# Prompt attention rows multiplied by their reciprocal sums on GpSimd instead of VectorE

## The chip, the cores and the metric

The kernel runs on one core of one Trainium2 chip. A core has a matrix engine (TensorE, PE in the profile), a vector engine (VectorE, DVE), an activation engine (ScalarE, ACT), GpSimd (POOL) and a queue engine for transfers (SyncE, SP). They run side by side and are tied together by semaphores only. The metric is the device time of one launch in microseconds. A time for comparison is a median of several runs; the profile is one more execution with the hardware profiler on.

## The reference

The program computes one inference step of a two-layer hybrid decoder for 512 prompt tokens and 8 samples of 8 tokens, all in float32. Each layer has three mixers (a causal pooling mixer, a gated linear recurrence and a latent attention), their gated merge, and a gated feed-forward network with a short convolution. The change touches one step of the attention of the prompt, eight heads over 512 tokens:

```python
s = einsum(q_lat, ckv) + einsum(q_pe, kpe)
s = where(q_pos >= k_pos, s * MLA_SCALE, -inf)
p = softmax(s, axis=-1)
o = einsum(p, ckv)
```

The softmax is computed as the maximum of a row, the exponential of the row less its maximum (with the sum of the row beside it), the reciprocal of the sum, and the product of the row with that reciprocal. The last product is the subject here.

## The kernel before

The prompt attention of a layer is cut into 32 blocks, numbered n = 0 to 31: four pairs of heads, four chunks of 128 queries in each pair, two heads in each chunk. Block n has 128 queries in the partitions and, because of the causal mask, 128, 256, 384 or 512 keys in the columns, two blocks of each width in turn. So the pattern of widths repeats every eight blocks, and a period here means eight blocks (one pair of heads).

Each block passes through these steps, with the program's names:

- TensorE makes the scores in PSUM (`att_score`, L930 and L931 for the mask).
- VectorE takes the negative maximum of each row out of PSUM (`att_stats`, L2035).
- ScalarE writes the exponentials to `probs`, one of four SBUF buffers (`r` in the profile), and the row sums to `stat` (`att_softmax`, L1632).
- VectorE takes the reciprocal of the sums, 128x1 (L2043), and multiplies the row by it, in place (L2045). Both are in `att_normalise`.
- TensorE transposes the row in pieces of 128 columns (`att_turn`, L939). ScalarE copies the result to SBUF (`att_take`, L1623). TensorE multiplies it with the values (`att_values`, L951), for two blocks at a time.

The order on each engine is written out by hand and never changes at run time. TensorE runs, for each n: scores of block n+3, transposes of block n, and after each odd n the values of the blocks two and three before. VectorE runs, for each n: reciprocal and product of block n, row maxima of block n+3; after n = 10, 18 and 26 it also copies a finished pair of heads out of PSUM (L2050). ScalarE runs: exponentials of block n, copy of the transposes of block n-2. An engine that waits for a semaphore holds up all that stands behind it.

The product signals `att_probs`, for which the transposes of the same block wait, and which a reciprocal four blocks later waits for too. GpSimd has nothing to do in this stage: its queue holds a subtraction (L2810) ahead of it, and behind it the first product of the recurrence (`value_blocks`, L2682), which waits for work after the attention of the samples. The sample attention follows the prompt attention on TensorE and has its own product on VectorE (L2265), which stays.

Of the kernel before, what the change touches and what calls it, by code (L numbers as in the profile page):

```python
# [20 lines left out]
ALU = mybir.AluOpType  # L21
# [4 lines left out]
P = 128  # L26
# [34 lines left out]
N_ATT_BUFS = 4  # L61
N_CHUNK = SEQ // CHUNK
# [114 lines left out]
N_ATT = MLA_HEADS * N_CHUNK  # L177
# [20 lines left out]
def build(nc, xT_in, w_stream, small_in, att_in, const_in, pages_in, kpe_in, page_table, pool_state,  # L198
          hgrn_state, conv_state, yT, ckv_out, kpe_out, pool_out, hgrn_p_out, hgrn_s_out, conv_out):
    with ExitStack() as ctx:  # L200
# [56 lines left out]
        probs = [r1[:, o + i * SEQ:o + (i + 1) * SEQ] for i in range(N_ATT_BUFS)]  # L257
# [142 lines left out]
        def att_stat(n, which):  # L400

            c = 4 * (n % N_ATT_BUFS) + which
            return stat[:, c:c + 1]
# [63 lines left out]
        def signal(name, per_layer):  # L467
            return Signal(sem(name), per_layer)
# [56 lines left out]
        att_recip = signal("att_recip", N_ATT)  # L525
        att_probs = signal("att_probs", N_ATT)
# [141 lines left out]
        def level_differences(eng, h, first=0, end=len(LEVELS)):  # L668

            for half, out, t0, t1 in levels(h, first, end):  # L670
                lo, hi, _ = parts(out, half)
                _, lhi, mid = parts(logf[:, h, t0:t1], half)
                alo, _, _ = parts(log_k[:, h, t0:t1], half)
                mid = mid.broadcast_to([P, (t1 - t0) // (2 * half), half])
                eng.tensor_tensor(hi, lhi, mid, ALU.subtract)
                ins = eng.tensor_tensor(lo, alo, mid, ALU.add)
            return ins

        def level_scaled(eng, h, first=0, end=len(LEVELS)):

            for half, out, t0, t1 in levels(h, first, end):
                _, hi, _ = parts(out, half)
                _, qhi, _ = parts(q_hg[:, h, t0:t1], half)
                ins = eng.tensor_tensor(hi, hi, qhi, ALU.mult)
            return ins
# [1301 lines left out]
        def _(dve):  # L1987
# [42 lines left out]
            def att_stats(l, n):  # L2030
                keys = (n % (2 * N_CHUNK) // 2 + 1) * P
                dve.wait_ge(*att_scores.at(l, n + 1))
                if n >= N_ATT_BUFS:
                    dve.wait_ge(*att_exp.at(l, n - N_ATT_BUFS + 1))
                dve.tensor_reduce(att_stat(n, 0), att_bank(n)[:, 0:keys], AX_X, ALU.max, negate=True  # L2035
                                  ).then_inc(att_max.sem, 1)

            def att_normalise(l, n):
                keys = (n % (2 * N_CHUNK) // 2 + 1) * P
                dve.wait_ge(*att_exp.at(l, n + 1))  # L2040
                if n >= N_ATT_BUFS:
                    dve.wait_ge(*att_probs.at(l, n - N_ATT_BUFS + 1))
                dve.reciprocal(att_stat(n, 3), att_stat(n, 2)).then_inc(att_recip.sem, 1)  # L2043
                dve.wait_ge(*att_recip.at(l, n + 1))
                dve.tensor_scalar(probs[n % N_ATT_BUFS][:, 0:keys], probs[n % N_ATT_BUFS][:, 0:keys], att_stat(n, 3), None,  # L2045
                                  ALU.mult).then_inc(att_probs.sem, 1)

            def take_head_pair(l, j):
                dve.wait_ge(*att_pv.at(l, N_CHUNK * (j + 1)))
                dve.tensor_copy(o_mla[:, j, 0:SEQ], pv_bank(j)).then_inc(att_out_taken.sem, 1)  # L2050
# [84 lines left out]
            with dve.Fori(0, DEPTH) as l:  # L2135
# [105 lines left out]
                        dve.tensor_copy(v_hg[0:rows, m, :], slot(TILE_HI + m)[0:rows, 0:512]).then_inc(tile_dve.sem, 1)  # L2241

                for n in range(N_ATT):
                    att_normalise(l, n)
                    if n + N_ATT_BUFS - 1 < N_ATT:
                        att_stats(l, n + N_ATT_BUFS - 1)

                    if n >= 10 and n % (2 * N_CHUNK) == 2:
                        take_head_pair(l, n // (2 * N_CHUNK) - 1)
# [410 lines left out]
        def _(pool):  # L2660
# [14 lines left out]
            def ends_scaled(l, h):  # L2675
                pool.wait_ge(*ends_exp.at(l, h + 1))
                pool.tensor_tensor(decayed[:, h % 2, 0, :], decayed[:, h % 2, 0, :], q_hg[:, h, :], ALU.mult
                                   ).then_inc(lev_ready.sem, 1)

            def value_blocks(l, h):  # L2680

                pool.tensor_tensor(v_blocks,  # L2682
                                   v_hg[0:SAMPLES, 4, h * P:(h + 1) * P].unsqueeze(1).broadcast_to(
                                       [SAMPLES, S_PAIRS, P]),
                                   own_rows.unsqueeze(2).broadcast_to([SAMPLES, S_PAIRS, P]), ALU.mult
                                   ).then_inc(blocks_ready.sem, 1)
# [119 lines left out]
            with pool.Fori(0, DEPTH) as l:  # L2806

                pool.wait_ge(*prep_dve.at(l, 8))
                pool.wait_ge(*q_rope.at(l, 2))
                pool.tensor_tensor(log_k, log_k, logf, ALU.subtract).then_inc(log_k_ready.sem, 1)  # L2810

                pool.wait_ge(*smp_new_rows.at(l, 2))
                pool.wait_ge(*smp_cols_taken.at(l, S_PAIRS))
                pool.wait_ge(*tile_act.at(l, taken(TILE_HQ + 3)))
                pool.wait_ge(*taken_at(l, TILE_HI + 4))
                pool.wait_ge(*log_k_ready.at(l, 1))
                value_blocks(l, 0)
                pool.wait_ge(*pool_d_ready.at(l, POOL_GROUPS))
                differences(l, 2)

                pool.wait_ge(*hg_upd.at(l, N_CHUNK + 2))
                ends(l, 2)
                value_blocks(l, 1)
                ends_scaled(l, 2)
                differences(l, 3)

                pool.wait_ge(*hg_upd.at(l, 2 * (N_CHUNK + 2)))
                ends(l, 3)
                value_blocks(l, 2)
                ends_scaled(l, 3)  # L2830

# [301 lines left out]
```

## Time and profile before

| | |
|---|---|
| median of 3 runs | 2267.76 us (2265.02 to 2270.11) |
| the profiled execution, its own time | 2267.23 us |
| span of the profiled execution | 2265.4 us |
| mean granted clock of TensorE | 0.994 |
| TensorE busy | 2196.5 us, 97% of the span |
| VectorE busy | 1183.0 us, 52% |
| GpSimd busy | 993.9 us, 44% |
| ScalarE busy | 526.5 us, 23% |

The span runs from the first to the last instruction; the launch adds 1.8 us around it. TensorE has work nearly always, so a change can move the time in two ways: by TensorE's own work, or by the gaps in which it waits. The prompt attention runs from about 158 to 209 us in the first layer and from about 1282 to 1333 us in the second. All stamps below are microseconds from the start of the span.

### The profile page before, as it was taken

To read this page: it belongs to the slowest core of one execution; us is meant where nothing else is said; L and a number is where in the kernel's file an instruction comes from. 1 tells how busy PE (TensorE), PEld (TensorE's weight loads), DVE (VectorE), ACT (ScalarE), POOL (GpSimd) and SP (SyncE) were. 2 spreads that over 40 slices of the span, in tenths; PEclk is the share of its full clock that TensorE was granted. 3 is DMA by queue.
4 is the path that set the end of the run, shared out by engine and by line. 5 is a ranking of instruction groups with operands and counts; after the bars stand their busy time and mean duration, and the time that the engine had idled before them with its cause. 6 is when DMAs were issued, how large, how long until landed. Compare 5 with 4: busy or idle time off the path is not lost.

```text
span 2265.4 us, 36978 instructions
## 1 busy us (share of the span) xinstructions
PE 2196.5 (97%) x11856; PEld 1691.6 (75%) x11856; DVE 1183.0 (52%) x2124; ACT 526.5 (23%) x1112; POOL 993.9 (44%) x1128
## 2 busy tenths in 40 slices
PE   8999999999999999999899999999999999999996
PEld 6775777777777777777676757777777777777775
DVE  0545666333578666661216346753335776666523
ACT  1434343111132001100134343531111311001002
POOL 0000046667665666633300000465666566666251
PEclk9999999999999999999999999999999999999998
DMA  5322113222132222222132221131221322222211
GB/s 210 101 84 66 43 63 114 84 75 77 55 126 75 74 76 88 71 72 77 38 133 86 75 67 42 63 133 66 84 84 57 120 80 74 74 74 70 96 52 42
DMA packets 51616, 183.54 MB, mean 81 GB/s; under 512 B 7234, under 2 KB 27970, under 8 KB 37762
## 3 DMA queue, kind: packets, MB, share of 16 engines
q1 hardware_dynamic: 50882, 178.49, 22.9%
q10 hardware_dynamic: 576, 3.06, 0.3%
q8 instruction: 84, 1.38, 0.2%
q14 instruction: 74, 0.61, 0.1%
HBM read 172.35 MB, written 9.18 MB: 80 GB/s over the span
## 4 chain that ended last, share of the span: by engine, by line
PE 91%; DVE 3%; issue 2%; POOL 1%; ACT 1%; SPq 1%; DMA 0%; DVEq 0%; ACTq 0%
PE ps L1219 25%; PE ps L1139 22%; PE ps L1261 16%; PE ps L898 12%; PE ps L1513 3%; PE ps L930 1%; PE ps L1427 1%; PE ps L1291 1%; PE ps L951 1%; PE ps L939 1%; PE ps L919 1%; PE ps L1079 1%; PE ps L983 1%; PE ps L1413 1%; PE ps L1057 1%
## 5 line engine op out<-in xcount | busy, mean ns | idle before, releaser
L1219 PE MATMUL ps<-lq,mreg 128*128 128x288 f32 x1008 | 251.3, 406 | 0.0
L898 PE MATMUL ps<-xT,wring 128*128 128x288 f32 (+2 forms) x960 | 236.5, 408 | 2.7 <-DVE o_mla L2289 1.4
L1219 PEld LDWEIGHTS ps<-lq,mreg 128*128 128x128 f32 x1008 | 191.5, 190 | 52.9
L1623 ACT ACTIVATE r<-ps 128x288 f32<-128x288 f32 (+7 forms) x264 | 112.8, 431 | 480.1 <-PE ps L1139 257.0
L898 PEld LDWEIGHTS ps<-xT,wring 128*128 128x128 f32 x960 | 183.2, 191 | 54.4 <-issue 2.2
L1219 PE MATMUL ps<-xT,wring 128*128 128x288 f32 x672 | 169.8, 406 | 0.0
L1219 PEld LDWEIGHTS ps<-xT,wring 128*128 128x128 f32 x672 | 127.7, 190 | 35.3
L1139 PE MATMUL ps<-r,kbuf 128*128 128x288 f32 x576 | 143.6, 406 | 0.0
L1139 PEld LDWEIGHTS ps<-r,kbuf 128*128 128x128 f32 x576 | 109.4, 190 | 30.2
L1952 ACT ACTIVATE r<-r 128x592 f32<-128x592 f32 x44 | 30.7, 697 | 428.5 <-DVE r L2594 428.5
L2783 POOL TENSOR_TENSOR kbuf<-o_mla 128x288 f32<-128x288 f32 x42 | 33.3, 792 | 207.8 <-DVE o_mla L2558 207.8
L1623 ACT ACTIVATE o_mla<-ps 128x288 f32<-128x288 f32 (+1 forms) x108 | 45.2, 420 | 326.2 <-PE ps L1261 214.5
L2810 POOL TENSOR_TENSOR kbuf<-kbuf,lq 128x2304 f32<-128x2304 f32 x2 | 10.1, 5054 | 248.4 <-DVE side L2221 248.4
L2682 POOL TENSOR_TENSOR mreg<-vbuf,const 64x512 f32<-64x512 f32 x8 | 8.3, 1032 | 251.8 <-PE ps L1541 243.1
L2594 DVE SCALAR_TENSOR_TENSOR r<-r,small 128x592 f32<-128x592 f32 x88 | 106.4, 1209 | 12.4 <-DVE r L2591 12.0
L2591 DVE SCALAR_TENSOR_TENSOR r<-r,small 128x592 f32<-128x592 f32 x88 | 104.5, 1188 | 12.4 <-DVE r L2588 9.7
L1139 PE MATMUL ps<-xT,wring 128*128 128x288 f32 x384 | 97.0, 406 | 0.0
L1261 PE MATMUL ps<-r,side 128*128 128x288 f32 x372 | 92.7, 407 | 0.8 <-DVE r L2605 0.8
L1219 PE MATMUL ps<-lq,wring 128*128 128x288 f32 x336 | 88.3, 406 | 0.0
L1219 PE MATMUL ps<-xT,mreg 128*128 128x288 f32 x336 | 88.3, 406 | 0.0
L1139 PEld LDWEIGHTS ps<-xT,wring 128*128 128x128 f32 x384 | 73.0, 190 | 20.2
L1139 PE MATMUL ps<-lq,r 128*128 128x288 f32 x336 | 87.4, 406 | 0.0
(435 smaller groups left out, 4540.6 us busy)
## 6 DMA issues: line engine op xcount, KB each, us to landing
wring<-w_stream SPq DMA_DIRECT2D x100, 1024.0 KB, 4.9
side<-w_stream SPq DMA_DIRECT2D x18, 704.0 KB, 4.5
r<-pages_in SPq DMA_DIRECT2D x80, 128.0 KB, 2.2
vbuf<-w_stream SPq DMA_DIRECT2D x12, 512.0 KB, 3.7
r<-w_stream SPq DMA_DIRECT2D x12, 512.0 KB, 3.6
wring<-w_stream SPq DMA_DIRECT2D x8, 704.0 KB, 4.1
r<-w_stream SPq DMA_DIRECT2D x6, 704.0 KB, 4.1
mreg<-pages_in SPq DMA_DIRECT2D x32, 128.0 KB, 2.1
```

Source lines behind the costliest of these rows:

```text
L898: mm = pe.matmul(out[0:w.shape[-1], a * 512:a * 512 + hi - lo], w, x[:, lo:hi], start=(k == 0), stop=(k == len(pairs) - 1))
L919: mm = pe.matmul(slot(tile + j)[:, a * 512:a * 512 + hi - lo], w, xT[:, k, lo:hi], start=(k == 0), stop=(k == KD - 1))
L930: pe.matmul(att_bank(n)[:, 0:keys], q96[:, j, e, t0:t0 + P], k96[:, j, e, 0:keys], start=True, stop=False)
L1139: mm = pe.matmul(banks[name], ws[:, k * P:(k + 1) * P], xs[:, k, :], start=(k == 0), stop=(k == n - 1))
L1219: mm = pe.matmul(up_sum[name], ws[:, k * P:(k + 1) * P], xs[:, k, :], start=(k == 0), stop=(k == HK - 1))
L1261: mm = pe.matmul(res_bank(which, m, i - 1), ws[:, k * P:(k + 1) * P], x, start=(k == 0), stop=(k == len(xs) - 1))
L1513: mm = pe.matmul(slot(TILE_HI + m)[g:g + rows, part * 256:(part + 1) * 256], xT[:, k, m * P:m * P + rows], w_slot[part][:, k * 256:(k + 1) ...
L1623: return act.activation(out, in_, func, **more)
L1952: act.activation(conv_h[u][0][:, 0:CX - 2], conv_h[u][0][:, 0:CX - 2], ACT.Silu).then_inc(silu_done.sem, 1)
L2591: dve.scalar_tensor_tensor(out=out, in0=src[:, 1:CX - 1], scalar=scalar(col + 2 * KF), in1=out, op0=ALU.mult, op1=ALU.add).then_inc(conv_s ...
L2594: dve.scalar_tensor_tensor(out=out, in0=src[:, 2:CX], scalar=scalar(col + 4 * KF), in1=out, op0=ALU.mult, op1=ALU.add).then_inc(conv_done. ...
L2783: pool.tensor_tensor(up_v[u], up_u2[u], up_p5s[u], ALU.add).then_inc(up_v_ready.sem, 1)
```

## The change

The product of a row with its reciprocal moves from VectorE to GpSimd. On VectorE it was an operation of a tensor with a per-partition scalar; on GpSimd it is a product of two tensors, the second of which is the 128x1 column of reciprocals, broadcast over all columns. The reciprocal stays on VectorE, together with its wait for the product four blocks before. GpSimd waits for each reciprocal (`att_recip`) and signals `att_probs` as VectorE did.

```diff
-            def att_normalise(l, n):
-                keys = (n % (2 * N_CHUNK) // 2 + 1) * P
+            def att_reciprocal(l, n):
                 dve.wait_ge(*att_exp.at(l, n + 1))
                 if n >= N_ATT_BUFS:
                     dve.wait_ge(*att_probs.at(l, n - N_ATT_BUFS + 1))
                 dve.reciprocal(att_stat(n, 3), att_stat(n, 2)).then_inc(att_recip.sem, 1)
-                dve.wait_ge(*att_recip.at(l, n + 1))
-                dve.tensor_scalar(probs[n % N_ATT_BUFS][:, 0:keys], probs[n % N_ATT_BUFS][:, 0:keys], att_stat(n, 3), None,
-                                  ALU.mult).then_inc(att_probs.sem, 1)
...
                 for n in range(N_ATT):
-                    att_normalise(l, n)
+                    att_reciprocal(l, n)
                     if n + N_ATT_BUFS - 1 < N_ATT:
                         att_stats(l, n + N_ATT_BUFS - 1)
...
+            def att_normalise(l, n):
+
+                keys = (n % (2 * N_CHUNK) // 2 + 1) * P
+                pool.wait_ge(*att_recip.at(l, n + 1))
+                row = probs[n % N_ATT_BUFS][:, 0:keys]
+                pool.tensor_tensor(row, row, att_stat(n, 3).broadcast_to([P, keys]), ALU.mult).then_inc(att_probs.sem, 1)
...
                 pool.tensor_tensor(log_k, log_k, logf, ALU.subtract).then_inc(log_k_ready.sem, 1)
+
+                for n in range(N_ATT):
+                    att_normalise(l, n)
```

In VectorE's queue before, at the start of the stage (`vbuf` is the value matrix of the recurrence, `stat` holds maxima, sums and reciprocals, `r` is the row of exponentials), this is the order:

```order
L2238 TENSOR_TENSOR vbuf<-ps,vbuf 64x512
L2043 RECIPROCAL stat<-stat 128x1
L2045 TENSOR_SCALAR r<-r,stat 128x128
L2032 REGISTER_ALU
L2035 TENSOR_REDUCE stat<-ps 128x1
L2043 RECIPROCAL stat<-stat 128x1
L2045 TENSOR_SCALAR r<-r,stat 128x128
L2032 REGISTER_ALU
L2035 TENSOR_REDUCE stat<-ps 128x1
```

The same place in VectorE's queue after the change:

```order
L2234 TENSOR_TENSOR vbuf<-ps,vbuf 64x512
L2042 RECIPROCAL stat<-stat 128x1
L2032 REGISTER_ALU
L2035 TENSOR_REDUCE stat<-ps 128x1
L2042 RECIPROCAL stat<-stat 128x1
L2032 REGISTER_ALU
L2035 TENSOR_REDUCE stat<-ps 128x1
```

Reciprocals and row maxima now alternate, with no product between them; nothing else moved on VectorE.

GpSimd's queue after the change, from the subtraction ahead of the stage on (`kbuf` and `lq` hold the recurrence's logarithms):

```order
L2813 TENSOR_TENSOR kbuf<-kbuf,lq 128x2304
L2679 ISA
L2681 TENSOR_TENSOR r<-r,stat 128x128
L2679 REGISTER_ALU
L2681 TENSOR_TENSOR r<-r,stat 128x128
L2679 REGISTER_ALU
L2681 TENSOR_TENSOR r<-r,stat 128x256
```

The 32 products of a layer stand between that subtraction and the first product of the recurrence. The queues of TensorE, ScalarE and SyncE are the same as before.

## Rows read from the trace of the kernel before

**Rows 1.** The page's part 4: the chain that ended last, by engine.

```profile
PE 91%; DVE 3%; issue 2%; POOL 1%; ACT 1%; SPq 1%; DMA 0%; DVEq 0%; ACTq 0%
```

**Rows 2.** Windows: stage and sample attention; columns are named in the first row.

```profile
core 0: us, PE busy (x) PEld busy (x) DVE busy (x) ACT busy (x) POOL busy (x), PEclk, DMA share, GB/s
158.40:208.70 50.30, 46.45 (x328) 33.11 (x328) 30.56 (x96) 29.19 (x89) 0.00 (x0) 1.00 0.27 89
234.00:246.00 12.00, 8.82 (x114) 6.91 (x112) 4.25 (x8) 3.69 (x9) 0.35 (x1) 1.00 0.08 23
```

**Rows 3.** TensorE's waits over the whole span: us in total, times, longest.

```profile
PE ps L939 <- DVE r L2045: 7.6, 14, 1.0
```

**Rows 4.** VectorE's timeline, blocks 11 to 17: start us, duration us, what, idle before.

```profile
175.82 0.35 DVE L2045 TENSOR_SCALAR r<-r,stat 128x256 f32<-128x256 f32 x1
176.09 0.68 DVE L2035 TENSOR_REDUCE stat<-ps 128x1 f32<-128x512 f32 x1
...
178.36 0.69 DVE L2035 TENSOR_REDUCE stat<-ps 128x1 f32<-128x512 f32 x1 [1.06 <-PE ps L931]
178.97 0.15 DVE L2043 RECIPROCAL stat<-stat 128x1 f32<-128x1 f32 x1
179.16 0.42 DVE L2045 TENSOR_SCALAR r<-r,stat 128x384 f32<-128x384 f32 x1
179.49 0.28 DVE L2035 TENSOR_REDUCE stat<-ps 128x1 f32<-128x128 f32 x1
...
179.88 0.49 DVE L2045 TENSOR_SCALAR r<-r,stat 128x512 f32<-128x512 f32 x1
...
181.84 0.49 DVE L2045 TENSOR_SCALAR r<-r,stat 128x512 f32<-128x512 f32 x1
...
185.26 0.29 DVE L2045 TENSOR_SCALAR r<-r,stat 128x128 f32<-128x128 f32 x1
```

**Rows 5.** TensorE's timeline, the transposes of blocks 11, 13, 14, 15 and 17.

```profile
176.23 0.44 PE L939 MATMUL ps<-const,r 128*128 128x128 f32 x2 [0.41 <-DVE r L2045]
...
179.63 0.55 PE L939 MATMUL ps<-const,r 128*128 128x128 f32 x3 [0.54 <-DVE r L2045]
...
181.24 0.60 PE L939 MATMUL ps<-const,r 128*128 128x128 f32 x4
...
182.38 0.66 PE L939 MATMUL ps<-const,r 128*128 128x128 f32 x4
...
185.61 0.33 PE L939 MATMUL ps<-const,r 128*128 128x128 f32 x1
```

**Rows 6.** From VectorE to GpSimd and back, in the merge (L2463, L2870, L2471).

```profile
435.12 0.45 DVE L2463 TENSOR_TENSOR r<-r,ps 128x288 f32<-128x288 f32 x1 [3.27 <-PE ps L1139]
435.65 0.79 POOL L2870 TENSOR_TENSOR r<-r 128x288 f32<-128x288 f32 x1 [4.78 <-DVE r L2463]
487.66 0.79 POOL L2870 TENSOR_TENSOR r<-r 128x288 f32<-128x288 f32 x1 [2.76 <-DVE r L2463]
488.56 0.46 DVE L2471 TENSOR_TENSOR r<-r,ps 128x288 f32<-128x288 f32 x1 [0.49 <-POOL r L2870]
```

**Rows 7.** GpSimd with a broadcast operand (L2682, L675), timeline.

```profile
245.65 1.03 POOL L2682 TENSOR_TENSOR mreg<-vbuf,const 64x512 f32<-64x512 f32 x1 [121.52 <-PE ps L1541]
...
295.77 0.62 POOL L675 TENSOR_TENSOR r<-lq 128x256 f32<-128x256 f32 x1
```

**Rows 8.** GpSimd with two full operands (L2840): duration ns, least, median, most.

```profile
L2840 POOL TENSOR_TENSOR kbuf<-wring x24: 1266/1267/1276, 356.9 to 1704.9; 128x512 f32<-128x512 f32 x24
...
L2840 POOL TENSOR_TENSOR r<-r x12: 717/722/728, 388.0 to 1718.6; 128x256 f32<-128x256 f32 x12
```

**Rows 9.** GpSimd and VectorE at once, both on SBUF tensors (L2847, L2509), timeline.

```profile
427.82 1.26 DVE L2509 TENSOR_TENSOR mreg<-mreg,side 128x576 f32<-128x576 f32 x1
428.42 1.24 POOL L2847 TENSOR_TENSOR r<-r 128x256 f32<-128x256 f32 x1
```

**Rows 10.** Block 3 at the start of the stage: its product, its transposes.

```profile
162.16 0.35 DVE L2045 TENSOR_SCALAR r<-r,stat 128x256 f32<-128x256 f32 x1
162.80 0.38 PE L939 MATMUL ps<-const,r 128*128 128x128 f32 x2
```

## The prediction, on record before the changed kernel was run

> **What bounds the kernel now.** I read the chain of the whole span first. TensorE holds 91% of it [rows 1], so what counts is TensorE's work and the gaps in front of it. The change leaves TensorE's queue alone; only gaps can move. Then I read the busy time of the stage: of 50.3 us TensorE is busy 46.45, VectorE 30.56, GpSimd 0 [rows 2]. No engine but TensorE is near full, so the question is one of latency and not of load. TensorE's list of waits names the product that moves: L939, the transposes, waited 7.6 us for L2045 in 14 places [rows 3]. That list understates it, since a wait hidden behind the modelled end of a matmul doesn't show. The two timelines side by side show more: for each odd block the transposes begin 0.05 us after the product ends. Block 11: product 175.82 + 0.35 = 176.17, transposes 176.23. Block 13: 179.16 + 0.42 = 179.58, then 179.63. Block 15: 181.84 + 0.49 = 182.33, then 182.38. Block 17: 185.26 + 0.29 = 185.55, then 185.61 [rows 4, 5]. Two of these show no idle time, and yet TensorE starts exactly when the product lets it. Even blocks have room: the product of block 14 ends at 179.88 + 0.49 = 180.37 and its transposes begin at 181.24, 0.87 us later [rows 4, 5].
>
> The reason is the written order. Before an even block's transposes TensorE has the values of two blocks to do; before an odd block's it has only the previous transposes and one set of scores. VectorE, for its part, can't touch the reciprocal of odd block n before it has reduced the scores of block n+2, for which it waits itself (1.06 us for the reduce at 178.36 [rows 4]). So the odd blocks run in a loop: scores, reduce, reciprocal, product, transposes. A longer product comes straight out of TensorE's time.
>
> **What the change does, part by part.**
>
> Removed from VectorE: 64 products. They shorten its queue, but the reduces that lead the loop waited for TensorE, so an earlier VectorE brings nothing there. I count 0.
>
> Added to the loop: the hops. Before, the product starts 0.04 us after the reciprocal (178.97 + 0.15 = 179.12, then 179.16), and TensorE 0.05 us after the product [rows 4, 5]. VectorE to GpSimd takes 0.08 us (435.12 + 0.45 = 435.57, then 435.65), and GpSimd to a waiting engine 0.11 us (487.66 + 0.79 = 488.45, then 488.56) [rows 6]. The loop gets 0.19 instead of 0.09 us: 0.10 us more per odd block.
>
> Changed in the loop: the duration of the product. On VectorE it takes 0.29, 0.35, 0.42 and 0.49 us for 128, 256, 384 and 512 columns, in sum 1.55 [rows 4]. On GpSimd this operation doesn't exist in the trace, so I bound it. Products and sums with an operand that is broadcast over many columns: 0.62 us for 256 and 1.03 for 512, the latter on 64 partitions [rows 7]. The line through both has 1.60 ns per column, which gives 0.41 for 128 and 0.83 for 384: sum 2.89. With two full operands: 0.722 for 256 and 1.267 for 512 [rows 8], so 2.13 ns per column, 0.45 for 128 and 0.99 for 384: sum 3.43. The new operand is a single column broadcast over the row, so the first pair is nearest and I take it; the second is the upper end. Below the first pair no row stands, but nothing excludes a gain from a one-column operand; the nearest bound is VectorE's own 1.55, at which only the hops would be left, 0.40 x 8 = 3.2 us. I leave 40% of the cost, between these two, for it in the range.
>
> Here the Trainium skill speaks against the change: "GPSIMD Engine Reference", section "Engine selection", sends elementwise work to VectorE because GpSimd is about twice as slow with two inputs, and its section "Performance versus the Vector engine" has a measured ratio of 1.96. The trace says 1.03 against 0.49 us, a ratio of 2.1 at 512 columns by the broadcast row and 2.6 by the full one, so it agrees in direction. By the page's 1.96 the four products would sum to 3.04 us and the result would be about 2282 us, an estimate that nothing below uses.
>
> Per odd block: 128 columns 0.41 - 0.29 + 0.10 = 0.22; 256: 0.62 - 0.35 + 0.10 = 0.37; 384: 0.83 - 0.42 + 0.10 = 0.51; 512: 1.03 - 0.49 + 0.10 = 0.64 us. One period has one odd block of each width: 1.74 us. Four periods make 6.9 us. One correction: block 3 has room, since its product ended at 162.51 and its transposes began at 162.80, 0.24 us more than the hop [rows 10]. So 6.7 us per layer and 13.4 us for two layers. The second layer's stage has the same code and the same loop.
>
> The even blocks must stay covered. On GpSimd the product of block 14 follows that of block 13 directly and ends 1.03 us after it. TensorE then has 181.24 - 179.63 = 1.61 us of transposes, values and scores between the starts of blocks 13 and 14 [rows 5]. Cover remains, about 0.6 us. If it failed in one even block of each period, at 0.2 us, it would cost 1.6 us in all. The load on GpSimd is small: four periods of two products of each width are 23 us in a stage of 50.3 us [rows 2]. GpSimd's later work isn't moved: it stood idle 121.52 us before 245.65, waiting for L1541 [rows 7], and the last product is done near 215. The reciprocal's own wait is for the product four blocks back, long done. The stage after the prompt attention shifts as a whole.
>
> The clock: the stage's granted clock is 1.00, and it is 1.00 too in the sample attention, where TensorE is busy only 8.82 of 12 us [rows 2]. With the added gaps the stage would be busy 46.45 of 57.0 us, 81%, which is more than those 74%. I count 0.
>
> Sum: 2267.23 us, the profiled execution's own time, plus 13.4 is 2280.6. That execution lies 0.5 us below the median of the runs (2267.76), so for a median I say 2281.0.
>
> **The rivals.**
>
> *Full price.* A broadcast column is read like any other tensor. Four products sum to 3.43 us; a period costs 3.43 - 1.55 + 0.40 = 2.28, eight periods 18.2, less 0.5 for block 3, plus some 0.6 where even blocks at the end of a layer, with no scores between them, lose cover: 18.3 us, 2286 us. For it: two tensor operands. Against it: both rows with a broadcast operand are shorter.
>
> *Contention.* GpSimd and VectorE get in each other's way. In the merge a 256-column sum took 1.24 us instead of 0.72 beside a VectorE sum of two SBUF tensors [rows 8, 9], a factor of 1.7. With it on the full price: 5.8 - 1.55 + 0.40 = 4.7 per period, 37 us, 2305 us. Against it: in this stage VectorE keeps reduces and copies that read PSUM and 128x1 reciprocals. "SBUF — State Buffer" of the Trainium skill, section "Who interferes with whom", says that a VectorE instruction contends only with two SBUF inputs or in a two-port mode; the slow row is of the first kind, so the trace agrees.
>
> *Nothing shows.* TensorE's queue hides the longer product, as it does for even blocks: 2267 to 2269 us. For it: only 14 waits and 7.6 us are on the list. Against it: the four starts 0.05 us behind the product.
>
> *Faster.* VectorE's queue is what delays the loop: the reduces at 176.09 and 179.49 stand right behind the products of blocks 11 and 13, with no idle time [rows 4]. If these reduces led to TensorE's gaps, they would come forward by 0.35 and 0.42 us per period, 6.2 us in eight: 2261 us. It decides once GpSimd's 384-column product and hops take no more than VectorE's 0.42 + 0.09 us. The broadcast rows say 0.83, and the reduces that lead the gaps waited for TensorE.
>
> **How the numbers follow.** Forecast 2281, chance 0.61. Full price 0.22, contention 0.06, nothing shows 0.07, faster 0.04. The forecast's own range is 2277 to 2285: a third of the 13.4 us less, and the even blocks' 1.6 us and half of the way to the full price more. The range for 8 in 10 takes in the full price and a shade beyond: 2275 to 2290. About 0.2%, 4.5 us, is what a measurement of this kernel can tell from no change. Slower by more: the first three, 0.89; within it 0.07; faster 0.04.
>
> **What the new profile would show.** GpSimd products at 0.4, 0.6, 0.8 and 1.0 us in the stage; TensorE's transposes of odd blocks 0.1 us behind them, even blocks later than their products; the stage 57.0 us long instead of 50.3 [rows 2]; everything after it equal in length. A stage of 59.5 us would be the full price; stretched products beside reduces would be contention. Products under 0.5 us at 384 columns, or odd transposes that don't follow them, would make the forecast wrong.

## The result, and the profile after

The changed kernel is slower: 2282.39 us, median of 4 runs (2280.36 to 2286.19), against 2268.51 us of the kernel before, a ratio of 1.0065 with a 95% interval of 1.0053 to 1.0078. The forecast was 2281 us. A second set of runs (e4 below) gave 1.0051, 1.0036 to 1.0066. The loss is 13.9 and 12.7 us by the medians, 14.7 and 11.6 us by the ratios: 12 to 15 us.

The page's part 1 of the changed kernel answers to the busy times of the table before: TensorE has the same 11856 matmuls, VectorE has 64 instructions fewer and GpSimd 64 more.

```profile
PE 2203.6 (97%) x11856; PEld 1696.0 (74%) x11856; DVE 1163.8 (51%) x2060; ACT 526.2 (23%) x1112; POOL 1039.4 (46%) x1192
```

The chain that ended last (part 4) answers to [rows 1]: TensorE's share fell from 91 to 80%, GpSimd's rose from 1 to 3%, VectorE's from 3 to 4%. The 10% of "issue" is time in which an engine of the chain waited for nothing that the profile shows. It isn't the price of the change: e1 below has the same 10% and is hardly slower than the kernel before.

```profile
PE 80%; issue 10%; DVE 4%; POOL 3%; ACT 1%; SPq 1%; DMA 1%; DVEq 0%; POOLq 0%; ACTq 0%
```

GpSimd's groups by shape (line, operation, shapes, count, busy us, mean ns, idle before). The four widths take 401, 614, 827 and 1041 ns, 2.88 us in sum.

```profile
L2681 POOL TENSOR_TENSOR r<-r,stat 128x512 f32<-128x512 f32 x16 | 16.6, 1041 | 7.9 <-DVE stat L2042 7.9
L2681 POOL TENSOR_TENSOR r<-r,stat 128x384 f32<-128x384 f32 x16 | 13.2, 827 | 17.5 <-DVE stat L2042 17.5
L2681 POOL TENSOR_TENSOR r<-r,stat 128x256 f32<-128x256 f32 x16 | 9.8, 614 | 21.9 <-DVE stat L2042 21.9
L2681 POOL TENSOR_TENSOR r<-r,stat 128x128 f32<-128x128 f32 x16 | 6.4, 401 | 86.3 <-DVE stat L2042 86.3
```

TensorE's list of waits over the whole span (us in total, times, longest) answers to [rows 3]: the transposes now wait for GpSimd, 22 times and 16.2 us.

```profile
PE ps L939 <- POOL r L2681: 16.2, 22, 1.4
```

TensorE's timeline of the changed kernel, the transposes of blocks 11 to 15, answers to [rows 5]:

```profile
179.82 0.44 PE L939 MATMUL ps<-const,r 128*128 128x128 f32 x2 [0.71 <-POOL r L2681]
181.74 0.49 PE L939 MATMUL ps<-const,r 128*128 128x128 f32 x3
183.66 0.55 PE L939 MATMUL ps<-const,r 128*128 128x128 f32 x3 [0.98 <-POOL r L2681]
185.28 0.60 PE L939 MATMUL ps<-const,r 128*128 128x128 f32 x4
187.02 0.66 PE L939 MATMUL ps<-const,r 128*128 128x128 f32 x4 [0.48 <-POOL r L2681]
```

and GpSimd's timeline beside it, the products of blocks 11, 12, 13 with 14 (merged into one row), 15 and 16:

```profile
179.16 0.61 POOL L2681 TENSOR_TENSOR r<-r,stat 128x256 f32<-128x256 f32 x1 [2.48 <-DVE stat L2042]
179.99 0.83 POOL L2681 TENSOR_TENSOR r<-r,stat 128x384 f32<-128x384 f32 x1 [0.22 <-DVE stat L2042]
182.78 1.83 POOL L2681 TENSOR_TENSOR r<-r,stat 128x384 f32<-128x384 f32 x2 [1.97 <-DVE stat L2042]
185.92 1.04 POOL L2681 TENSOR_TENSOR r<-r,stat 128x512 f32<-128x512 f32 x1 [1.31 <-DVE stat L2042]
187.15 0.40 POOL L2681 TENSOR_TENSOR r<-r,stat 128x128 f32<-128x128 f32 x1 [0.18 <-DVE stat L2042]
```

The transposes of these odd blocks begin 0.05 or 0.06 us after their products (179.16 + 0.61 = 179.77, then 179.82; 185.92 + 1.04 = 186.96, then 187.02), and block 15's wait, which [rows 5] hid, has come into view. The same holds for every odd block of the layer but block 3 (0.12 us). Block 12's product ends at 180.82, its transposes begin at 181.74: even blocks are covered. The exceptions are blocks 2 and 4 at the start of the stage, whose transposes begin 0.06 us after the product (block 2's did so before the change too); e2 shows that they cost nothing in the end.

To measure the stage I take two fixed points of TensorE's queue: the scores of block 3, which wait for the value matrix (L2238 before, L2234 after), and the first scores of the sample attention (L983). In the kernel before, on TensorE's timeline:

```profile
158.43 0.70 PE L930 MATMUL ps<-r 128*128 128x256 f32 x2 [1.48 <-DVE vbuf L2238]
...
209.45 1.94 PE L983 MATMUL ps<-r,side 128*64 128x512 f32 x8
```

and in the changed kernel:

```profile
160.22 0.70 PE L930 MATMUL ps<-r 128*128 128x256 f32 x2 [1.48 <-DVE vbuf L2234]
...
216.96 1.89 PE L983 MATMUL ps<-r,side 128*64 128x512 f32 x8
```

That is 51.02 us before and 56.74 after, 5.72 us more. The second layer has 51.03 and 56.74. So the stage accounts for 11.4 us, 0.50%. The spans differ by 16.0 us (2281.4 - 2265.4); the other 4.6 us lie outside the stage, and experiment e4 takes them up.

What one period costs can be read from the same blocks eight apart. Block 21, before and after:

```profile
193.12 0.55 PE L939 MATMUL ps<-const,r 128*128 128x128 f32 x3 [0.54 <-DVE r L2045]
...
198.66 0.55 PE L939 MATMUL ps<-const,r 128*128 128x128 f32 x3 [0.98 <-POOL r L2681]
```

From block 13 to block 21 the kernel before takes 193.12 - 179.63 = 13.49 us, the changed one 198.66 - 183.66 = 15.00: 1.5 us more in a period, where the prediction had 1.74.

### The profile page after: what moved, and what is told of

It reads as the page before. It is cut to its first block, busy times and chain, and to the rows that moved or that the text cites. A ratio compares the mean times of both kernels' runs of the same rounds, so it can differ in the third digit from the quotient of the medians.

```text
span 2281.4 us, 37038 instructions
## 1 busy us (share of the span) xinstructions
PE 2203.6 (97%) x11856; PEld 1696.0 (74%) x11856; DVE 1163.8 (51%) x2060; ACT 526.2 (23%) x1112; POOL 1039.4 (46%) x1192
## 4 chain that ended last, share of the span: by engine, by line
PE 80%; issue 10%; DVE 4%; POOL 3%; ACT 1%; SPq 1%; DMA 1%; DVEq 0%; POOLq 0%; ACTq 0%
PE ps L1219 25%; PE ps L1139 21%; PE ps L1261 16%; PE ps L898 8%; POOL r L2681 2%; PE ps L1427 1%; PE ps L1291 1%; PE ps L1079 1%; PE ps L919 1%; PE ps L983 1%; PE ps L1025 1%; PE ps L1057 1%; PE ps L1413 1%; DMA wring<-w_stream 1%; POOL kbuf L2813 0%
## 5 line engine op out<-in xcount | busy, mean ns | idle before, releaser
L2681 POOL TENSOR_TENSOR r<-r,stat 128x128 f32<-128x128 f32 (+3 forms) x64 | 45.7, 721 | 133.7 <-DVE stat L2042 133.7
```

The lines of the kernel that those rows point to most:

```text
L2681: pool.tensor_tensor(row, row, att_stat(n, 3).broadcast_to([P, keys]), ALU.mult).then_inc(att_probs.sem, 1)
```

## The experiments

The theory under test is the loop: only the product of an odd block stands between the scores of block n+2 and the transposes of block n. The rivals are that any product's time counts, and that GpSimd at work costs something by itself. All stage lengths are between the two fixed points above, in the first layer.

**e1, short odd products.** The product of odd blocks covers only the first 128 columns; the rest of those rows stays unnormalised.

```diff
+                if n % 2 == 1:
+                    keys = P
                 row = probs[n % N_ATT_BUFS][:, 0:keys]
```

> The changed kernel, but the GpSimd product of each odd block covers its first 128 columns only (the rest of those rows stays unnormalised); even blocks keep the full width. Loop theory: only odd blocks stand in the loop scores, reduce, reciprocal, product, transposes. With 0.40 us for each odd product instead of 0.40, 0.61, 0.83 and 1.04 the stage should lie about 1 us per layer above the kernel before, instead of 5.7: some 2 us in all, 2270 to 2272 us. Rival, any product counts: half of the added product time is taken away, so about half of the 14 us stays, 2275 us. Rival, GpSimd at work in this stage is itself the cost (clock or port): nearly all stays, 2280 us or more.

Measured: 2270.11 us, ratio 1.0003 (0.9994 to 1.0012), which can't be told from no change; the stage is 52.00 us, 0.98 more than before. GpSimd still did 64 products, the even ones at full width and cost.

**e2, short even products.** The same with `n % 2 == 0`.

> The mirror of the other: the GpSimd product of each even block covers its first 128 columns only, odd blocks keep the full width. Loop theory: even products are covered by TensorE's values and scores, so the stage stays where the changed kernel has it, at most 0.5 us per layer less: 2281 to 2283 us, and the transposes of odd blocks still wait 1.0 us and more. Rival, any product counts: about half of the 14 us goes, 2275 us.

Measured: 2279.97 us, ratio 1.0050 (1.0037 to 1.0063), stage 56.26 us, 5.24 more than before and 0.48 less than with the whole change. TensorE's list of waits in this kernel:

```profile
PE ps L939 <- POOL r L2683: 15.9, 20, 1.4
```

By the page GpSimd is busy 1028.7 us here and 1028.8 us in e1, against 1039.4 us with the whole change: the same 10.7 us, over both layers, are taken away in both. In e1 this brings the stage of one layer 4.74 us down, here 0.48. Together e1 and e2 rule out both rivals: where the product stands decides, not how much GpSimd works.

The 0.48 us come from the end of the stage. Counted from the fixed point, the transposes of blocks 5 to 30 begin in e2 within 0.02 us of where they begin in the changed kernel; those of block 31, the last, begin at 54.99 us instead of 55.44. With the full width GpSimd's product of block 31 has to wait for that of block 30: it starts 0.86 us after its reciprocal, in e2 0.22.

**e3, VectorE padded.** No GpSimd in the stage; the kernel before with one more VectorE operation in front of each product.

```diff
                 dve.reciprocal(att_stat(n, 3), att_stat(n, 2)).then_inc(att_recip.sem, 1)
+                dve.tensor_reduce(att_stat(n, 1), probs[n % N_ATT_BUFS][:, 0:keys], AX_X, ALU.max)
                 dve.wait_ge(*att_recip.at(l, n + 1))
```

> The kernel before, product on VectorE, with one more VectorE operation between reciprocal and product of each block: a maximum over the row of exponentials in SBUF, written to an unused column (about 0.21, 0.34, 0.48 and 0.61 us for the four widths). GpSimd idle in the stage as before. Loop theory: latency counts and not the engine, so the stage grows by 6 to 7 us per layer, 12 to 14 us in all, 2280 to 2283 us. Rival, GpSimd at work is the cost: no change, 2268 us. If dips of TensorE's granted clock outside the stage come with the shift of the work in time and not with GpSimd, this profile should show other dips than the kernel before as well.

Measured: 2277.47 us, ratio 1.0040 (1.0027 to 1.0053), stage 55.15 us, 4.13 more. The direction is as the loop has it, the size is not the 6 to 7 us expected. VectorE's timeline of this kernel shows why, here for block 13:

```profile
179.77 0.15 DVE L2043 RECIPROCAL stat<-stat 128x1 f32<-128x1 f32 x1
179.84 0.53 DVE L2044 TENSOR_REDUCE stat<-r 128x1 f32<-128x384 f32 x1
180.29 0.41 DVE L2046 TENSOR_SCALAR r<-r,stat 128x384 f32<-128x384 f32 x1
```

The added reduce overlaps the ends of its neighbours: from reciprocal to product it is 0.52 us instead of 0.19, so 0.33 added and not 0.48. The same reading for the four widths gives 0.06, 0.20, 0.33 and 0.46, in sum 1.05 us per period and 4.2 in four: the 4.13 measured. The expectation took durations where start-to-start distances count. With that, a slower engine and a longer queue on the fast engine have the same effect, and nothing is left for GpSimd's being at work as such.

**e4, the changed kernel again**, unchanged.

> The changed kernel once more, unchanged, for its spread and for the dips of TensorE's granted clock: 2280 to 2286 us, the stage 5.7 us longer per layer than before. If the dips outside the stage (at 253, 1359 and 1475 us in the first profile, 3.4 us each at half clock) belong to the change, they stand at the same places again; if they are chance, they move or vanish and the time moves by about 1.7 us for each.

Measured: 2281.28 us median of 6 runs (2275.71 to 2284.97), ratio 1.0051 (1.0036 to 1.0066), stage 56.74 us in both layers. A dip is a stretch in which the clock granted to TensorE falls to its lower level. The windows of the first profile of the changed kernel show one (us, busy times, granted clock, DMA share, GB/s):

```profile
250.00:253.00 3.00, 1.93 (x32) 1.19 (x27) 0.28 (x1) 0.56 (x2) 0.00 (x0) 1.00 0.30 81
253.00:257.00 4.00, 3.61 (x9) 2.91 (x10) 3.40 (x16) 0.00 (x0) 1.03 (x1) 0.58 0.02 7
```

TensorE had been busy 1.93 of 3 us at the end of the sample attention; then the clock was at its lower level, 1.2 GHz, for 3.4 us (the mean of 0.58 is 0.42 short over 4 us, and half clock is 0.5 short), and 1.7 us of work at full clock went missing. The table counts such stretches from windows of 1 us; one of 6.8 us counts as two, and the one between the layers (6.8 us long) and the one at the end, which all have, are left out, and so are e7 to e9, in which a dip lies within a stage:

| kernel | span less its two stages, us | dips of 3.4 us outside the stages |
|---|---|---|
| before | 2163.4 | 2 |
| e5 | 2161.2 | 2 |
| e2 | 2162.7 | 3 |
| e1 | 2164.3 | 3 |
| e3 | 2166.8 | 5 |
| e6 | 2166.8 | 4 |
| changed | 2167.9 | 5 |
| e4 | 2168.5 | 6 |

The time outside the stage grows with the number of dips, and 1.7 us for each fits the table as a whole. There is a scatter of 1 to 2 us besides: the two kernels with two dips differ by 2.2 us. So the 4.6 us of the first comparison are not simply three more dips, 5.1 us. By place they are (4.5 us in all, without the rounding of the spans):

- 1.8 us ahead of the first stage, which starts at 158.43 us before and at 160.22 after. There is no dip there in either; 1.0 us of it is TensorE's wait for the first weights, 9.9 us instead of 8.9. In e4 the same kernel has its first stage at 158.87.
- 1.6 us between the stages, with one dip more.
- 1.1 us behind the second stage, with two dips more.

Both profiles of the changed kernel have dips at 252 to 253, 1358 to 1359, 1385 to 1386 and 1474 to 1475 us, so they seem to stay with a program; e3, without GpSimd in the stage, has as many, so their number doesn't come from GpSimd's products. Two of them, this one and the one at 346 us in the kernel before (busy 2.23 of the 3 us ahead of it), stand just behind a stretch in which TensorE had gaps. Why one kernel draws more than another isn't settled here.

**e5, new order on VectorE, product on VectorE.** Reciprocal and product of the odd block come before the reduces.

```diff
                 for n in range(N_ATT):
-                    att_normalise(l, n)
+                    if n % 2 == 0:
+                        att_normalise(l, n)
+                        att_normalise(l, n + 1)
                     if n + N_ATT_BUFS - 1 < N_ATT:
                         att_stats(l, n + N_ATT_BUFS - 1)
```

> The kernel before with VectorE's order changed: reciprocal and product of blocks n and n+1 (n even), then the row maxima of blocks n+3 and n+4. The product of an odd block no longer stands behind the reduce of block n+2. Loop theory: TensorE's waits for the product, 1.27 us in each period of eight blocks, go almost entirely, 4.3 us per layer: about 8.5 us faster, 2260 us, with a period of 12.2 us. Rival, the exponentials are what is late (their chain through the copies on ScalarE): no gain, 2268 us, or slower since maxima come later.

Measured: 2257.34 us against 2267.71, ratio 0.9954 (0.9941 to 0.9968), stage 45.62 us, 5.40 less. This kernel beats both. The gain is larger than the 4.3 us per layer expected: the transposes of blocks 13 and 21 begin at 177.69 and 189.54, a period of 11.85 us instead of 13.49, so 1.64 us less and not 1.27. What the 0.37 us more are isn't settled here. TensorE's wait for the product has gone from 7.6 [rows 3] to this:

```profile
PE ps L939 <- DVE r L2045: 0.7, 2, 0.3
```

VectorE's timeline shows the products of two blocks of 256 columns next to each other, with the reduces before and behind:

```profile
171.76 0.56 DVE L2035 TENSOR_REDUCE stat<-ps 128x1 f32<-128x384 f32 x1 [0.55 <-PE ps L931]
172.23 0.15 DVE L2043 RECIPROCAL stat<-stat 128x1 f32<-128x1 f32 x1
172.42 0.35 DVE L2045 TENSOR_SCALAR r<-r,stat 128x256 f32<-128x256 f32 x1
172.69 0.15 DVE L2043 RECIPROCAL stat<-stat 128x1 f32<-128x1 f32 x1
172.88 0.35 DVE L2045 TENSOR_SCALAR r<-r,stat 128x256 f32<-128x256 f32 x1
173.95 0.56 DVE L2035 TENSOR_REDUCE stat<-ps 128x1 f32<-128x384 f32 x1 [0.72 <-PE ps L931]
```

The second product is done at 173.23, and its reader begins at 175.05 in TensorE's timeline:

```profile
175.05 0.38 PE L939 MATMUL ps<-const,r 128*128 128x128 f32 x2
```

The rival, late exponentials, is out: delaying the maxima by a product cost nothing.

**e6, new order on VectorE, product on GpSimd**: the same edit with `att_reciprocal`.

> The changed kernel with the same new order on VectorE: reciprocals of n and n+1, then the maxima of n+3 and n+4; products on GpSimd. Loop theory: the product leaves the loop, so its engine hardly matters: about 6 us below the kernel before, 2262 us, a period of 12.3 us and 1 us per layer more than the same order with VectorE's product. Rival, the product's duration counts wherever it stands: 11 to 14 us above the same order with VectorE's product, 2272 us or more.

Measured: 2260.38 us, ratio 0.9966 (0.9952 to 0.9979), stage 47.69 us: 3.33 below the kernel before and 2.07 above e5. Moving the product to GpSimd costs 4.1 us in both layers in this order instead of 11.4 (3.0 by the medians). That is twice the 1 us per layer expected, but far from the rival. The trace shows where part of it comes from. GpSimd's products of blocks 12 and 13 and of blocks 14 and 15 (merged into a row each), and the transposes of blocks 12 and 14:

```profile
177.20 1.61 POOL L2683 TENSOR_TENSOR r<-r,stat 128x384 f32<-128x384 f32 x2 [2.45 <-DVE stat L2042]
179.56 2.04 POOL L2683 TENSOR_TENSOR r<-r,stat 128x512 f32<-128x512 f32 x2 [0.74 <-DVE stat L2042]
...
178.09 0.55 PE L939 MATMUL ps<-const,r 128*128 128x128 f32 x3
...
180.65 0.66 PE L939 MATMUL ps<-const,r 128*128 128x128 f32 x4
```

Block 12's product takes 0.83 us and ends at 178.03, block 14's takes 1.04 and ends at 180.60; their transposes begin 0.06 and 0.05 us later. So in the even blocks of 384 and 512 columns the transposes now follow the product at once, and in the odd ones they have 0.10 and 0.20 us of room (blocks 13 and 15): the product hasn't left TensorE's path altogether.

**e7, e8, e9, a full second operand.** The column of reciprocals is replaced by a full tensor: by constants in e7, by constants with an addition in e8, by activations in e9. None of the three normalises the rows.

```diff
-                pool.tensor_tensor(row, row, att_stat(n, 3).broadcast_to([P, keys]), ALU.mult).then_inc(att_probs.sem, 1)
+                pool.tensor_tensor(row, row, cos[:, 0:keys], ALU.mult).then_inc(att_probs.sem, 1)
```

In e8 `ALU.mult` is `ALU.add`; in e9 `cos[:, 0:keys]` is `xT[:, 0, 0:keys]`.

> The changed kernel, but the second operand of the GpSimd product is a full tensor of constants (the rows are multiplied by the cosine table and not normalised). If a broadcast column is cheaper to read than a tensor, the products take 0.45, 0.72, 0.99 and 1.27 us instead of 0.40, 0.61, 0.83 and 1.04, and the stage grows by a further 2.5 us per layer, 5 us in all: 2287 us. If the operation costs the same either way: 2282 us and the same durations.

Measured in e7: 2280.81 us, ratio 1.0051 (1.0037 to 1.0065), so no slower than the changed kernel; in the second layer, which no dip touches, the stage is 57.26 us. Its products of 512 columns:

```profile
L2681 POOL TENSOR_TENSOR r<-r,const 128x512 f32<-128x512 f32 x16 | 17.4, 1091 | 7.6 <-DVE stat L2042 7.6
```

That is only 50 ns above the broadcast column, where 1267 ns had been expected from [rows 8], and neither of the two outcomes of the expectation. e8 and e9 ask for the reason:

> The kernel with the full second operand, but GpSimd adds the constant tensor instead of multiplying (no normalisation). It asks why a product of two full tensors took 1.09 us at 512 columns where the sums of the merge, on which the full price was built, take 1.27. If the operation makes the difference (a sum is dearer than a product), 1.27, 0.99, 0.72 and 0.45 us here and a stage 2.5 us longer per layer than the changed kernel's. If it is the place or the kind of the operands, 1.09 us again, and the same stage as with the full product.

> The kernel with the full second operand, with that operand taken from the tensor of activations instead of the constants (a product, no normalisation). If the address of the second operand sets the price, the durations move away from 0.41, 0.64, 0.86 and 1.09 us; if the product as an operation sets it, they stay.

Measured, one run each, so that their times (2283.30 and 2285.98 us, against 2273.81 for the kernel before) allow no verdict and only the durations count: e8 has 1090 ns at 512 columns, so a sum costs what a product costs. e9 has this:

```profile
L2681 POOL TENSOR_TENSOR r<-r,xT 128x512 f32<-128x512 f32 x16 | 20.2, 1269 | 6.5 <-DVE stat L2042 6.5
...
L2681 POOL TENSOR_TENSOR r<-r,xT 128x256 f32<-128x256 f32 x16 | 11.6, 725 | 21.1 <-DVE stat L2042 21.1
```

That is the price of [rows 8] to 3 ns, by the choice of the second tensor alone. Its stage in the first layer is 59.18 us, 8.16 more than before: the full-price rival made real. It would have been 16.3 us for two layers; the prediction had 18.3 for it. The stage bears the durations out: they are 0.56 us longer in four products than the changed kernel's, 2.2 us in four periods, and the stage is 2.44 us longer.

## Why the prediction was right

Step by step:

- *The bound.* TensorE and its gaps: right. TensorE's instructions are the same, and the gaps in front of the transposes grew. The reading of starts 0.05 us behind a product, where the list shows no wait, was the key: blocks 15 and 17 showed no idle time [rows 5] and yet paid.
- *The duration of the product.* 0.41, 0.62, 0.83 and 1.03 us forecast from [rows 7], 0.40, 0.61, 0.83 and 1.04 measured.
- *The hops.* The term that was mis-sized. VectorE to GpSimd is 0.08 us as forecast (on VectorE's timeline the reciprocal of block 13 ends at 182.55 + 0.15 = 182.70, the product starts at 182.78). GpSimd to TensorE is 0.05 us and not the 0.11 us that [rows 6] have for GpSimd to VectorE. So 0.04 us are added per odd block (0.08 + 0.05 for 0.04 + 0.05) and not 0.10. In a period that is 0.24 us less: 1.74 - 0.24 = 1.50, and 1.5 were measured from block 13 to 21. In four odd blocks of eight periods it is 1.9 us: 13.4 - 1.9 = 11.5, and the stages measured 11.4. The trace of the kernel before already shows that this time differs by the pair. Here VectorE begins 0.04 us after GpSimd ends (613.20 + 3.13 = 616.33, then 616.37):

```profile
613.20 3.13 POOL L2905 TENSOR_TENSOR mreg<-mreg,r 128x576 f32<-128x576 f32 x2 [1.00 <-DVE r L2509]
...
616.37 1.50 DVE L2488 TENSOR_TENSOR o_mla<-mreg 128x288 f32<-128x288 f32 x1 [2.65 <-POOL mreg L2905]
```

- *Even blocks* were covered, apart from 0.5 us per layer. e2 puts that at the last block alone, whose product waited for block 30's on GpSimd. In the kernel before, block 31 was not in the loop (its transposes began 0.43 us after its product), so the sum priced a block that had room and left out a queue that formed; the two partly cancel.
- *VectorE's shorter queue* brought nothing, as forecast: the period's 1.50 us are accounted for without it.
- *The clock.* In the stage of the changed kernel it stayed at 1.00, as forecast, but not by a safe margin: in e7 to e9, with a slightly longer stage, a dip falls into the end of one of the two stages and makes it about 1.1 us longer than the other (e7: granted clock 0.50 from 215.0 to 217.5 us). Outside the stage the forecast of nothing was wrong: the changed kernel's profiles have five and six dips, the kernel before has two. The whole loss less the stages' 11.4 us leaves 2.5 us (first set) and 1.3 us (e4) by the medians, 3.3 and 0.2 us by the ratios. The hops' surplus of 1.9 us and this remainder, which wasn't foreseen, work against each other, so that 2281 lies closer to 2282.4 than the working deserved; that is luck.
- *Nothing shows*, *contention* and *faster* are out. The products took the same time beside VectorE's reduces as the line through [rows 7] says. *Faster* named VectorE's queue as the delay, and e5 shows that it was one, but through the reduce in front of the odd product and not through the product in front of the reduce; moving the product's engine doesn't touch that.

## What to carry to other kernels

Before moving work to an idle engine, look at when its reader starts: if the reader begins a hop after the work ends, block after block, a longer piece of work delays the reader by as much, even where no wait is listed. Then look for what stands in front of the work on its own queue. Here putting one waiting instruction behind the product instead of ahead of it was worth 10 us, while relieving its engine of 25 us of products (16 of each width, 1.55 us for four) cost 12 to 15. A new order has to be read again with the engine in mind: in e6 the same move still cost 4.1 us, through other blocks.

## What the runs showed of the hardware that I had not expected

- A GpSimd operation on two float32 tensors costs 1.09 or 1.27 us at 512 columns depending on which tensor its second operand is (e7, e9), and the same for sum and product (e7, e8). What about the tensor does it, its address or something else, is open.
- The time from the end of a GpSimd operation to the start of what waits for it differs by the pair: 0.05 us to TensorE's transposes, 0.11 to VectorE's L2471 [rows 6], 0.04 to VectorE's L2488.
- TensorE's clock fell to half for 3.4 us at a time outside the stage, about 1.7 us of time each, two to six times in a run, at four common places in two profiles of one kernel.
